# The second expert weight's loads moved from SyncE's queue to ScalarE's, in a hybrid attention and mixture-of-experts layer

## What is computed

```python
def moe_ffn(h, w_router, b_router, w1, b1, w2, b2):
    top_vals, top_idx = lax.top_k(logits, TOP_K)              # 4 of 32 experts for each row
    ...
    def expert_block(args):
        xb, e = args
        hid = xb @ w1[e] + b1[e]                              # w1[e]: 1024 x 2048 float32, 8 MB
        return clamped_swiglu(hid) @ w2[e] + b2[e]            # w2[e]: 1024 x 1024 float32, 4 MB
    y = lax.map(expert_block, (x_rows, block_expert)).reshape(n_rows, D)
    return jnp.zeros_like(h).at[row_tok].add(y * row_gate[:, None])
```

## Time and profile before

| | us |
|---|---|
| median of 3 runs | 1420.99 (1419.43 to 1422.98) |
| the profiled execution's own time | 1421.71 |
| its span, first to last instruction | 1419.6 |
| TensorE busy (PE) | 1376.0 (97%) |
| VectorE busy (DVE) | 578.6 |
| ScalarE busy (ACT) | 241.6 |
| GpSimd busy (POOL) | 83.5 |

### The profile page before, as it was taken

The page is one execution under the profiler, slowest core; times in us unless marked ns, Lnnn a source line. Parts: engine busy times, 40 slices in busy tenths (PEclk is TensorE's granted clock), DMA queues, the critical chain, the costliest instruction groups (busy, mean ns, idle before and its releaser), DMA issues.

```text
span 1419.6 us, 29112 instructions
## 1 busy us (share of the span) xinstructions
PE 1376.0 (97%) x12142; PEld 675.7 (48%) x12142; DVE 578.6 (41%) x884; ACT 241.6 (17%) x514; POOL 83.5 (6%) x117
## 2 busy tenths in 40 slices
PE   7999999999999999999999999999999999999897
PEld 5887755553443343434434343434434343434466
DVE  5323356675333333343434343343343333333543
ACT  6423333312111100010101000010100000000322
POOL 7000000010000000000000000000000000000010
PEclk9999999989999999999999999999999999999999
DMA  5131250668999999999999999999999999999201
GB/s 184 60 119 60 100 226 16 228 202 329 367 369 387 409 396 410 409 409 411 411 408 408 408 403 409 410 407 409 409 407 398 408 411 407 408 404 395 86 5 56
DMA packets 72062, 445.56 MB, mean 314 GB/s; under 512 B 8003, under 2 KB 8566, under 8 KB 22854
## 3 DMA queue, kind: packets, MB, share of 16 engines
q1 hardware_dynamic: 68032, 434.01, 76.9%
q0 software_dynamic: 3360, 8.62, 2.1%
q10 hardware_dynamic: 614, 2.11, 0.4%
HBM read 443.13 MB, written 4.19 MB: 315 GB/s over the span
## 4 chain that ended last, share of the span: by engine, by line
PE 92%; issue 3%; DVE 3%; ACT 1%; DMA 0%; DVEq 0%; POOL 0%; ACTq 0%; POOLq 0%
PE ps L1235 40%; PE ps L1269 13%; PE ps L988 9%; PE ps L1261 7%; PE ps L1307 7%; PE ps L1020 3%; PE ps L1413 2%; PE ps L1208 1%; DVE XT L1621 1%; PE ps L1182 1%; PE ps L1292 1%; PE ps L1002 1%; PE ps L1081 1%; PE ps L1069 1%; PE ps L1281 1%
## 5 line engine op out<-in xcount | busy, mean ns | idle before, releaser
L1235 PE MATMUL ps<-W,XT 128*32 128x512 f32 x5184 | 576.3, 594 | 6.1 <-DVE XT L1621 6.1
L1235 PEld LDWEIGHTS ps<-W,XT 128*32 128x32 f32 x5184 | 169.5, 110 | 362.4 <-issue 362.3
L1664 DVE TENSOR_TENSOR H<-H,ps 128x1024 f32<-128x1024 f32 x124 | 146.1, 1218 | 342.5 <-PE ps L1307 342.5
L1269 PE MATMUL ps<-W,HIDT 128*32 128x256 f32 x3264 | 181.5, 381 | 4.9 <-DVE YL L1657 4.9
L1269 PEld LDWEIGHTS ps<-W,HIDT 128*32 128x32 f32 x3264 | 106.4, 111 | 83.2 <-issue 17.3
L801 ACT ACTIVATE SIG<-T 128x768 f32<-128x768 f32 (+1 forms) x32 | 23.8, 744 | 638.8 <-DVE T L1601 638.8
L1261 PE MATMUL ps<-W,HIDT 128*32 128x512 f32 x960 | 105.7, 592 | 0.0
L1621 DVE COPY XT<-ps 128x480 f32<-128x480 f32 (+1 forms) x64 | 28.7, 490 | 180.1 <-PE ps L1208 180.1
L574 POOL DMA_INDIRECT XG<-f_rows,row_of x33 | 33.8, 1024 | 895.5 <-PE ps L1208 885.2
L1307 PE MATMUL ps<-YH,OH 96*128 96x512 f32 (+1 forms) x248 | 70.6, 433 | 0.0
L1601 DVE TENSOR_SCALAR T<-ps 128x768 f32<-128x768 f32 (+1 forms) x32 | 26.7, 833 | 99.0 <-PE ps L1235 99.0
(11 more groups left out here) (321 smaller groups left out, 1294.1 us busy)
## 6 DMA issues: line engine op xcount, KB each, us to landing
W<-in_w_dram SPq DMA_DIRECT2D x384, 1024.0 KB, 19.9
wst<-in_w_in_dram SPq DMA_DIRECT2D x6, 2048.0 KB, 8.5
H<-in_x_dram SPq DMA_DIRECT2D x8, 512.0 KB, 4.8
wst<-in_w_out_dram SPq DMA_DIRECT2D x2, 2048.0 KB, 9.4
W<-in_w_ple_gate_dram SPq DMA_DIRECT2D x4, 1024.0 KB, 12.8
f_rows<-M ACTq DMA_DIRECT2D x4, 512.0 KB, 3.3
out_dram<-TL SPq DMA_DIRECT2D x4, 512.0 KB, 2.6
wst<-in_w_ple_proj_dram SPq DMA_DIRECT2D x1, 1024.0 KB, 5.0
```

What stands on the lines that cost most here:

```text
L1235: last = pe.matmul(ps[STRIP * q:STRIP * (q + 1), r], XT[:, k, STRIP * g:STRIP * (g + 1)], w_slot(k)[:, n * 512:(n + 1) * 512], start=False ...
L1269: last = pe.matmul(ps[STRIP * q:STRIP * (q + 1), bank, at:at + 256], HIDT[:, f, STRIP * g:STRIP * (g + 1)], w2j[:, ff * 1024 + n * 256:ff ...
L1664: dve.tensor_tensor(H[:, t], H[:, t], ps[:, bank:bank + 2].rearrange("p a n -> p (a n)"), ALU.add).then_inc(comb_added, 1)
```

## The change

The four loads of w2 leave SyncE's loop. ScalarE issues them at the start of its part of block b, from b = 2 on, all four together behind one wait that all four chunks of the previous w2 are used. `load_w2` takes the engine as an argument. ScalarE reads the expert's number from the table itself, and waits once for the table to be there (`count_ready`) ahead of block 2. The very last w2, which goes to slots 4 to 7, stays with SyncE.

```diff
-        def load_w2(sp, b, e):
+        def load_w2(eng, b, e):
+            eng.wait_ge(w2_used, b * 4)
             for j in range(4):
-                sp.wait_ge(w2_used, (b - 1) * 4 + (j + 1))
-                load_chunk(sp, NC + j, e)
+                load_chunk(eng, NC + j, e)
...
                 b = i + 2
-                before_e = sp.value_load(tab[0:1, bass.ds(b - 1, 1)], min_val=0, max_val=NE - 1)
                 e = sp.value_load(tab[0:1, bass.ds(b, 1)], min_val=0, max_val=NE - 1)
                 load_w1(sp, b, e)
-                load_w2(sp, b - 1, before_e)
...
             def expert_block(b, last, this, next, ple=None, second=False):
+                if not second:
+                    e = act.value_load(tab[0:1, bass.ds(b - 1, 1)], min_val=0, max_val=NE - 1)
+                    load_w2(act, b - 1, e)
                 choose_bias(b + 1, next, second=second)
...
             expert_block(1, False, False, True, second=True)
+            act.wait_ge(count_ready, 1)
```

## The result

| | before | after |
|---|---|---|
| median of the executions | 1421.53 us (1419.43 to 1422.98, 4) | **1434.91 us** (1431.65 to 1436.34, 4) |
| ratio, 95% interval | | 1.0092 (1.007 to 1.0114) |
| the profiled execution's own time | 1421.71 us | 1431.65 us |
| its span | 1419.6 us | 1429.4 us |

The change costs 13.4 us by the medians and 9.9 us between the two profiled executions.

What follows compares the result with a forecast made beforehand. It took TensorE and the DMA engines as both full, with no wait on weight loads. Waits of 6.0 us in twelve small blocks plus 2.7 us in block 4 made 8.7 us: 1429.7 us as median, range 1420 to 1446.

Steps and rivals of the forecast that it cites:

- likeliest case: Short TensorE waits on w2's last chunk in small blocks and block 4; 1424 to 1440 us, chance 0.52.
- rival 2: DMA engines become the bound because two read streams cost some of the 424 GB/s; 1435 to 1446 us, chance 0.10.
- SyncE's gain: SyncE loses four issues, four waits and a table read per block; nothing was late there, gain 0.
- ScalarE's own time: Table read, register work and four issues add 2.3 us per block, with over 20 us of cover; cost 0.
- the new wait: ScalarE's wait for four used chunks of previous w2, which YH's activation has just waited for; cost 0.
- When the loads go out: First w2 issue some 0.8 us after YH starts in a small block; first load 7.5 us later than before.
- The halves: w2's and w1's queues share the engines equally; w2 takes 21.8 us, landing at 771.6 us, wanted at 771.1.
- Block 4: Worst case, its own w2 part being the short one: TensorE waits 2.7 us, once.
- How often: The 0.5 us wait falls in twelve small blocks behind a large one, 6.0 us.
- w1 late: Chunk 7 of a small block lands at 759.3 us, wanted at 761.4; cost 0, bound 5 us in all.
- Rival 1: w2 lands before TensorE needs it, so nothing changes; 1421.7 to 1425 us, chance 0.35.
- The coarser grain: Engines might send a whole chunk before switching queues; last w2 chunk up to 2.5 us sooner, sum 0 to 8.7 us.

Runs made afterwards that it cites:

- The holds: TensorE held twice in block 5 until GpSimd finished meaningless additions: kernel before 1430.86 us (+9.9), changed kernel 1440.65 us (+19.7).

## Why the prediction was right, and where it was not

- **The sign and the size of the whole** held: 1429.7 us forecast, 1434.91 measured, inside 1420 to 1446 and inside the likeliest case's 1424 to 1440. The range was wide, from no effect up; its upper end is rival 2's, since 1.5 us a block and block 4 make 1441.7. The forecast's own cost was 8.7 us, the measured one 13.4. The mechanism was the forecast one, TensorE waiting for w2's last chunk on a queue that shares its engines.
- **SyncE's gain 0, ScalarE's own time 0, the new wait 0**: right. 2.11 us of issue before 14.33 us of idle time. Later issue in SyncE's line: +0.
- **When the loads go out**: right, the issue follows YH's start by 0.8 us (493.19, 493.97).
- **The halves**: right. Where w2 and w1 start together the last landing is 24.2 us after the first issue, as forecast (24.3). In block 6 of the change it was 26.9: 2.6 us more. The first chunk tells where, 12.0 us beside a running w1 queue against 9.3 where both queues start on idle engines. So entering busy engines cost about one chunk's time more than halves alone, which the prediction had at nothing; what in the queues does that is open. It is why blocks 6 and 8 wait 3 us and not 0.5.
- **Block 4**: 2.7 us forecast, 2.1 measured.
- **"How often" is the term that failed.** It multiplied 0.5 us by twelve small blocks. Measured: 2.9 us in block 6, 3.1 in block 8, and nothing in the other ten. The prediction took a full w1 queue as given in every block. It even said that each us that TensorE waits elsewhere shortens this queue, but used that for w1 only. The backlog of seven chunks exists because TensorE has not yet waited; once it has lost 8 us, w1's queue is empty when w2 goes out, and the first chunk lands in 5.2 us, not 12.0. The holds show this from the other side. Where w2 goes out later still, the fixed difference does come in every small block, 18 waits in all. The sum of waits came near (8.0 against 8.7) because two errors met: fewer blocks, longer waits.
- **The clock was not in the sum.** 1.6 us of the 9.9 are the one row at the lower level. Behind the loop the execution loses 1.4 us more; it has another such stretch there (0.83 from 1360 to 1370 us, where the execution before had 1.00), behind a wait of 3.3 us that both executions have. The other three executions after have a mean granted clock of 0.987 to 0.988 and spans of 1432.3 to 1433.6 us, where the profiled one has 0.990 and 1429.4. For the 3.3 us from it to the median, its lucky start and the clock are the candidates, but no trace of those executions shows the place.
- **w1 late: cost 0, bound 5 us**: right for the change, but the margin of 2 us is as thin as it said (by its own terms the chunk lands at 749.4 + 5.7 + 3.8 = 758.9, not 759.3): with w2 issued early, or w1 held back, w1 is what comes late (4.8, 5.0, 3.7 us).
- **Rival 1, nothing changes**: wrong in blocks 4, 6 and 8, right in all the others, though not for its reasons. By the Trainium skill, *DMA: Bandwidth & Descriptors*, section on issuing engines that are no separate DMA queues, loads from several engines interleave on the same 16 engines and only issue time is saved. The trace agrees with the first part (share 1.01 and 405 to 407 GB/s with one queue or two). It differs on the second: interleaving is itself a change of order, and cost 0.9% here.
- **The coarser grain** fell. By the Trainium skill's same page, section on queues, rings and completion order, a packet, typically of 9 to 17 descriptors, is drained before a switch. The prediction took from it that a chunk of eight rows an engine goes at once. Then the chunks of the two queues would land 2.5 us apart; the four pairs landed 0.1 to 0.2 us apart (the fourth at 791.6 and 791.5). The engines switch within a chunk. The page of the changed kernel counts 17894 packets for the 127.94 MB of q10, 7.1 KB each on average, so by its count a packet is about one row; whether that is the skill's packet, no run here shows.
- **Rival 2, the engines become the bound**: its time (1435 to 1446) lies nearer to 1434.91 than my 1429.7 does, but its signs are absent: no wait in large blocks, 405 to 407 GB/s in a pair as before, 425 GB/s with both queues busy. A reader with the time alone could have taken it for the right one.

## What to carry to other kernels

When the engines and the consumer are both full, the order in which loads are served matters and the number of queues doesn't. One queue filled in the order of use is a schedule by deadline; a second queue turns it into equal shares, and a load with little to spare then lands a few us late. Before such a move, list for each load when it lands and when it is wanted, and recompute the backlog after the first wait: it may be a price paid once, not one per iteration. But if the issue is so late that the shared transfer alone takes longer than TensorE's way to the chunk (24.2 us against 22.2 here), it is paid in every block. And don't expect a repair from making loads wait for loads: behind the first or second chunk it won nothing over one queue, behind the fourth it left pauses and cost 82 us.

## What the runs showed of the hardware that was not expected

- **A wait of TensorE of about 2 to 3 us can cost more than itself.** 48 matmuls behind the wait of 2.18 us took 4.43 us instead of 2.80 (granted clock 0.58 over those 4 us); the wait of 2.19 us in block 6 had no such effect. In the holds the granted clock was 0.57 in both stretches:

```profile
470.00:474.00 4.00, 3.91 (x24) 1.07 (x28) 0.00 (x0) 0.00 (x0) 0.03 (x1) 0.57 1.01 420
490.00:498.00 8.00, 5.10 (x28) 1.29 (x32) 0.80 (x1) 0.00 (x0) 2.53 (x5) 0.57 0.75 302
```

  7.4 us of holds cost 9.9 us. It is not certain each time: the kernel before has the wait of 3.3 us behind its loop too, and no slow matmuls there.
- **The steepness.** One chunk of w1 later cost 34 us more than the change, three chunks later 119 us more, in waits of about 2 us in every block and in clock (13.9 and 49.6 us more of TensorE busy time than before). On one queue, loads 1.5 to 5.1 us later than before cost nothing.
